# Two transformer blocks on one core: one pass over x for two norm roots, context prepared inside a feed-forward, index scores ordered by head

## The reference, cut to what matters

```python
# block 1
x = x + 0.5 * swiglu(rmsnorm(x, g_ffn1), ...)                     # ffn1
p = rmsnorm(x, g_mix) @ w_in                                      # qa, ka, va, qi, ki, wi, cq, ckv, kr
# index scores: 16 heads of 64 features, three blocks of 128 queries with 256, 384, 512 keys
idx_logits = einsum('bqhd,bsd->bqhs', qib, k_idx)
score = einsum('bqh,bqhs->bqs', wb, relu(idx_logits))             # top-k of it selects keys
q = rmsnorm(c_q, g_q_lat) @ w_uq ; kv = rmsnorm(c_kv, g_kv_lat) @ w_ukv   # value half of kv: VB
out_a = sparse attention (8 heads) ; out_b = latent attention (8 heads)
x = x + concat([out_a, out_b]) @ w_out
x = x + 0.5 * swiglu(rmsnorm(x, g_ffn2), ...)                     # ffn2
x = rmsnorm(x, g_final)                                           # "final"
# block 2
x  = x  + 0.5 * ml[2] * swiglu_2(modulate(rms_norm(x,  norm1_g), ml[0], ml[1]), ...)   # ffn3
cx = cx + 0.5 * mc[2] * swiglu_2(modulate(rms_norm(cx, norm1_g), mc[0], mc[1]), ...)   # same weights
# projections, convolution branch, attention of 8 heads over 768 keys, merge, last feed-forward
```

## Time and profile before

| | us |
|---|---|
| median of 3 runs | 2821.77 (2820.44 to 2825.56) |
| the profiled execution | 2822.73 |
| its span, first to last instruction | 2820.9 |
| mean granted TensorE clock over the span | 0.959 |
| PE busy | 2709.4 |

### The profile page before, as it was taken

One profiled execution on the slowest core, in us unless ns is written; L12 is line 12 of the kernel. 1 busy time (PEld: TensorE's weight loads), 2 busy tenths in 40 slices (PEclk: granted clock), 3 DMA queues, 4 the chain that ended last, 5 costly groups with the idle time before them and its releaser, 6 DMA issues.

```text
span 2820.9 us, 34194 instructions
## 1 busy us (share of the span) xinstructions
PE 2709.4 (96%) x12500; PEld 2168.7 (77%) x12500; DVE 1421.5 (50%) x2491; ACT 757.6 (27%) x1029; POOL 346.7 (12%) x259
## 2 busy tenths in 40 slices
PE   8999989888899999998999999999999999999998
PEld 6888877644457888878888888878888756888887
DVE  7877784556647756673122222254324653433333
ACT  3111232235542112133111111222322352321213
POOL 2111120000002101111211301200200002210102
PEclk9999999869699999987999999999999999999999
DMA  6444432200034454431212221222332001323331
GB/s 181 135 134 144 135 116 74 54 15 1 0 102 115 135 142 147 130 109 37 67 60 60 60 75 56 64 75 90 90 105 83 31 1 60 90 90 98 96 97 67
DMA packets 394763, 241.12 MB, mean 85 GB/s; under 512 B 14768, under 2 KB 392752, under 8 KB 394672
## 3 DMA queue, kind: packets, MB, share of 16 engines
q1 hardware_dynamic: 394672, 239.92, 29.1%
HBM read 237.79 MB, written 2.10 MB: 85 GB/s over the span
## 4 chain that ended last, share of the span: by engine, by line
PE 88%; DVE 7%; ACT 4%; issue 1%; DMA 1%; POOL 0%; SPq 0%; DVEq 0%; ACTq 0%; POOLq 0%
PE PS L669 22%; PE PS L676 21%; PE PS L671 21%; PE PS L656 3%; PE PS L653 3%; PE PS L654 3%; PE PS L1053 2%; PE PS L810 1%; PE PS L610 1%; DVE RB L1414 1%; PE PS L1033 1%; PE PS L896 1%; DVE WL L1361 1%; PE PS L876 1%; PE PS L903 1%
## 5 line engine op out<-in xcount | busy, mean ns | idle before, releaser
L669 PE MATMUL PS<-NH,WH 128*128 128x512 f32 (+1 forms) x2128 | 626.0, 376 | 10.6 <-DVE WL L1361 6.3
L671 PE MATMUL PS<-NH,WL 128*128 128x512 f32 (+1 forms) x2128 | 620.1, 373 | 0.0
L676 PE MATMUL PS<-NL,WH 128*128 128x512 f32 (+1 forms) x2128 | 591.5, 372 | 0.0
L1361 DVE TENSOR_TENSOR WL<-RAW,WH 128x2048 fp32r<-128x2048 f32 x190 | 462.0, 2432 | 103.6 <-ACT WH L1080 103.1
L1080 ACT ACTIVATE WH<-RAW 128x2048 fp32r<-128x2048 f32 x190 | 363.7, 1914 | 540.0 <-PE PS L676 501.0
L669 PEld LDWEIGHTS PS<-NH,WH 128*128 128x128 f32 x2128 | 384.0, 189 | 79.3 <-issue 9.0
L671 PEld LDWEIGHTS PS<-NH,WL 128*128 128x128 f32 x2128 | 389.3, 189 | 72.2
L676 PEld LDWEIGHTS PS<-NL,WH 128*128 128x128 f32 x2128 | 389.5, 189 | 71.9
L1414 DVE SCALAR_TENSOR_TENSOR RB<-MW,CV,RB 128x128 f32<-128x128 f32 x826 | 329.2, 431 | 17.8
L1126 ACT ACTIVATE SA<-PS 128x512 f32<-128x512 f32 x104 | 62.0, 596 | 663.1 <-PE PS L676 630.6
L669 PE MATMUL PS<-HH,WH 128*128 128x512 f32 (+1 forms) x820 | 237.5, 371 | 1.9 <-DVE WL L1361 1.9
(11 more groups left out here) (268 smaller groups left out, 2691.6 us busy)
## 6 DMA issues: line engine op xcount, KB each, us to landing
RAW<-in_ffn_w_in SPq DMA_DIRECT2D x88, 512.0 KB, 4.8
MW<-in_w_mod SPq DMA_DIRECT2D x72, 512.0 KB, 3.7
RAW<-in_w_in SPq DMA_DIRECT2D x70, 512.0 KB, 4.1
RAW<-in_w_gate SPq DMA_DIRECT2D x44, 512.0 KB, 4.2
RAW<-in_w_up SPq DMA_DIRECT2D x44, 512.0 KB, 5.4
RAW<-in_w_down SPq DMA_DIRECT2D x32, 512.0 KB, 4.3
RAW<-in_ffn_w_out SPq DMA_DIRECT2D x32, 512.0 KB, 4.3
RAW<-in_w_out SPq DMA_DIRECT2D x16, 512.0 KB, 4.4
```

The source lines that it names most:

```text
L669: pe.matmul(outs[half][x], w[half][0], xh(k), start=k == 0, stop=False)
L671: pe.matmul(outs[half][x], w[half][1], xh(k), start=False, stop=False)
L676: last = pe.matmul(outs[half][x], w[half][0], xl(k), start=False, stop=k == kn - 1)
L1361: dve.tensor_tensor(WL[1 - s][:, :], RAW[1 - s][:, :], WH[1 - s][:, :].bitcast(F32), ALU.subtract).then_inc(w_lo, 1)
```

## The change

1. *Index scores.* `INDEX` runs over heads outside and the three blocks of queries inside. The products use four banks, the relus three slices of SA. The roots of `norm_q` and `norm_kv` are taken together, their squares during the last projection stages; their spreads stand after index products 2 and 3. VectorE applies both norms and splits the value weights before its first index sum. The value product stands inside the index products, one token block after each of products 24, 26, 28 and 30, in banks 4 and 6, and ScalarE copies it to VB. The clearing of VB and the KB copies go to GpSimd, early.
2. *Between the blocks.* `norm_final` is gone. With y = x r g, the root that ffn3 needs is that of y: ScalarE squares each slice twice, once scaled by the absolute gain (for `norm_x1`, with eps2 = eps squared), once plain (FS); GpSimd adds both. `norm_x1` reads the X of ffn2 with the gain GX. The plain sum gives the final norm's root later: its sums stand after the spread of `norm_x1`, its root after the third high half, its spread before the seventh slice of ffn3's first stage, and VectorE multiplies X by it (`final_applied`) in that stage, with the rest of the `b_mod` additions.
3. *Context.* The squares (two activations with an accumulated sum), transposes, copies and root of the context run in the first four `down` stages of ffn2 (`ctx_work`), its scaling and halves one slice per stage in the second `gate_up` chunk. These stages are written out instead of looped.
4. *Attention.* The value products of a group stand after the scores and before the turn of the next group's first unit, in both attentions.
5. SBUF tiles are placed anew (VB behind QB and KB; FS and FD over unused parts of the hidden tiles).

```diff
+        INDEX = [(q, h) for h in range(IDX_HEADS) for q in range(1, NT)]
+        IX_V = 24
 # TensorE
-            norm(norm_q, v_b)
-            norm(norm_kv, None)
...
+            norm_sums(norm_q, None)
+            norm_sums(norm_kv, None)
+            pe.wait_ge(psum_free, v_b)
+            for n, (q, h) in enumerate(INDEX):
+                if n >= 4:
+                    pe.wait_ge(ix_relu, n - 3)
+                r = slice((h % 2) * 64, (h % 2) * 64 + 64)
+                pe.matmul(B[n % 4][:, 0:(q + 1) * P], QI[r, h // 2, q * P:(q + 1) * P], KI[r, 0:(q + 1) * P],
+                          start=True, stop=True).then_inc(ix_mm, 1)
+                if n == 2:
+                    norm_spread(norm_q, None)
+                elif n == 3:
+                    norm_spread(norm_kv, None)
+                elif n >= IX_V and n % 2 == 0 and n < IX_V + 2 * NT:
+                    values((n - IX_V) // 2)
...
+                if u > 0 and u % PER_GROUP == 0:
+                    heads(u // PER_GROUP - 1)
                 if u >= 0:
                     turn(u)
-                    if u % PER_GROUP == PER_GROUP - 1:
-                        heads(u // PER_GROUP)
+            heads(NG - 1)
...
-            norm(norm_final, ffn3[0][0])
-            pe.wait_ge(ctx_loaded, 16 * (TC // P))
-            for n in range(2 * TC // P):
...
-            norm(norm_c1, None)
-            norm(norm_x1, None)
+            norm_sums(norm_x1, None)
+            norm_spread(norm_x1, ffn3[0][0])
+            pe.wait_ge(f_acc, KD - 1)
+            for t in range(NT):
+                last = pe.matmul(B[4][:, t:t + 1], FS[:, 0, t * P:(t + 1) * P], ones[:, 0:1], start=True, stop=True)
+            last.then_inc(f_mm, 1)
 # ScalarE
+            for n, (q, h) in enumerate(INDEX):
+                act.wait_ge(ix_mm, n + 1)
+                if n >= 3:
+                    act.wait_ge(ix_acc, n - 2)
+                act.activation(SF[:, (n % 3) * T:(n % 3) * T + (q + 1) * P], B[n % 4][:, 0:(q + 1) * P], ACT.Relu)\
+                    .then_inc(ix_relu, 1)
+                if n == 2:
+                    norm_high(norm_q)
+                    norm_high(norm_kv)
...
 # VectorE
+            norm_inverse(norm_q)
+            norm_inverse(norm_kv)
+            norm_apply(norm_q)
+            dve.wait_ge(norm_lo, norm_q.lo + 3)
+            norm_apply(norm_kv)
+            split(v_b % 2, v_b)
+            for n, (q, h) in enumerate(INDEX):
...
+            def final_applied():
+                dve.wait_ge(f_rb, 1)
+                for k in range(KD):
+                    last = dve.scalar_tensor_tensor(out=X[:, k, :], in0=X[:, k, :], scalar=vec("g_final", k), in1=RB[:, :],
+                                                    op0=ALU.mult, op1=ALU.mult)
...
             for b, j, s, at in stage(dve, b0, n, low is not None, lead=2 if b0 == ffn3[0][0] else 0):
+                    if low is not None:
+                        norm_scaled(low, j)
                     mods(b0, j, s, m0)
                     split(s, b)
+                    if low is not None:
+                        norm_low(low, j)
 # GpSimd
+            def final_sum(k):
+                pool.wait_ge(f_sq, k + 1)
+                if k > 1:
+                    pool.wait_ge(f_acc, k - 1)
+                pool.tensor_tensor(FS[:, 0, :], FS[:, 0, :], FS[:, 1 + k % 2, :], ALU.add).then_inc(f_acc, 1)
```

More of the change, by code:

```diff
@@ L622, in norm_spread @@
                         .then_inc(norm_bc, 1)
-                if warm_up:
+                if warm_up and m is not norm_x1:
                     busy(5)
@@ L779, in items, with values @@
                     last.then_inc(rope_mm, 1)
+            def values(t):
+                s = v_b % 2
+                if t == 0:
+                    begin(v_b)
+                    pe.wait_ge(norm_lo, norm_kv.lo + 2)
+                if t >= 2:
+                    pe.wait_ge(v_out, t - 1)
+                for k in range(2):
+                    xh, xl = (z[:, (3, 7)[k], t * P:(t + 1) * P] for z in (NH, NL))
+                    wh, wl = (z[s][:, k * 512:(k + 1) * 512] for z in (WH, WL))
+                    pe.matmul(B[4 + 2 * (t % 2)][:, :], xh, wh, start=k == 0, stop=False)
+                    pe.matmul(B[4 + 2 * (t % 2)][:, :], xh, wl, start=False, stop=False)
+                    last = pe.matmul(B[4 + 2 * (t % 2)][:, :], xl, wh, start=False, stop=k == 1)
+                last.then_inc(v_mm, 1)
             for n in range(10):
@@ new lines, in norm_low @@
+            def norm_low(m, k):
+                if k in m.pooled:
+                    return
+                dve.wait_ge(norm_hi, m.low + k + 1)
+                h, l = m.dst(k)
+                if m.shift:
+                    ins = dve.scalar_tensor_tensor(out=l, in0=scaled(m, k), scalar=m.shift(k),
+                                                   in1=h.bitcast(F32), op0=ALU.add, op1=ALU.subtract)
+                else:
+                    ins = dve.tensor_tensor(l, scaled(m, k), h.bitcast(F32), ALU.subtract)
+                ins.then_inc(norm_lo, 1)
@@ L1431, in gate_up @@
+            def gate_up(b0, n, tok, g0, h0, m0=None, low=None):
+                for b, j, s, at in stage(dve, b0, n, low is not None, lead=2 if b0 == ffn3[0][0] else 0):
+                    if low is not None:
+                        norm_scaled(low, j)
                     mods(b0, j, s, m0)
                     split(s, b)
+                    if low is not None:
+                        norm_low(low, j)
+                    if b0 == ffn3[0][0] and isinstance(j, int) and j == 0:
+                        final_applied()
@@ L1892, in _ @@
             ffn(ffn2, T, H0["ffn2"])
-            norm(norm_final)
+            norm(norm_x1)
+            final_sum(KD - 1)
+            pool.wait_ge(f_r, 1)
+            for t in range(NT):
+                pool.tensor_scalar(FD[:, t * P:(t + 1) * P], ident[:, :], RF[:, t:t + 1], None, ALU.mult).then_inc(f_dg, 1)
             ffn(ffn3, T + TC, H0["ffn3"])
```

356 lines of the change are left out of this document (210 added, 146 removed).

## The result

The changed kernel takes 2753.62 us (median of 4 runs, 2751.96 to 2756.46) against 2821.11 for the kernel before on the same chip: ratio 0.976, 95% interval 0.9743 to 0.9777. The forecast was 2749, so the gain is 68 us where 73 were expected. The profiled execution took 2751.96, its span is 2750.2.

What follows compares the result with a forecast made beforehand. PE, busy 96% of the span, bounds the kernel, so gains are its low-clock or idle time and removed work. 27 + 31 + 9 + 6 = 73 us off 2822.73 gives 2749.7, median 2749; range 2738 to 2758, chance 0.60.

Steps and rivals of the forecast that it cites:

- Part 1: Index scores up to ScalarE's weight copy for `project(0)`: a gain of 27 us, bounds a loss of 3 to 33.
- VectorE's pace: Index scores: VectorE alone needs 1.62 us a head, 26 us for 16 heads; taken for the last eight heads.
- I let the clock rise during it, and stay up: Index scores: PE's clock rises during the value product, from product 24, and stays up.
- the front: Start of the index scores: norm sums, first products and VectorE's norms and value weights put the first index sum at 558.2 us.
- Rival A: Index scores: a head's products run serially; gain 19 instead of 27, or -3; time 2757 to 2779; chance 0.16.
- Part 2: Between the blocks: one pass instead of three gains 36.5 us, net 31 after costs in ffn2 and ffn3; bounds 27 to 34.
- only that of slice 6: Between the blocks: of GpSimd's additions of squares only slice 6's is on the path, as in the kernel before.
- rival C: Feed-forward stages: hidden context and final norm work shows, 16 us come back, time 2765; chance 0.07.
- Part 3: Attentions: later value products fill PE's waits for PT; gains 9 us in block 1 and 6 in block 2.
- the upper bound of 20 for block 1: First attention: the gain could reach 20 us through fewer drops of the clock.
- Rival D: From the index scores on: half-filled array keeps the clock at 1.2 GHz, attentions start low; slower, 2889; chance 0.02.

Runs made afterwards that it cites:

- e10: Changed kernel with the value product from index product 38 on instead of 24: 2753.31 us, ratio 0.9766 to the kernel before.
- e5: Changed kernel with index products ordered so that neighbours are in alternate halves of the array: 2750.06 us, ratio 0.9741 to the kernel before.
- e7: Changed kernel with two banks instead of four for the index scores: 2783.90 us, ratio 0.9864 to the kernel before.
- e6: Changed kernel with 96 unused bytes ahead of HH, which then starts on a multiple of 128: 2743.36 us, ratio 0.9719 to the kernel before.
- e1: Kernel before with one unused tile of 32 bytes per partition ahead of HH, no instruction changed: 2833.77 us against 2819.65, ratio 1.0047.
- e9: Changed kernel with index products in alternating halves and 96 unused bytes ahead of HH: 2738.84 us, ratio 0.971 to the kernel before.
- e4: Changed kernel with the product of heads after the turn of its last unit again, in both attentions: 2776.25 us, ratio 0.9844 to the kernel before.

## Why the prediction was right, and where it was not

**Part 1** (-27, measured -26.1). All times here count from the last projection product. The first index sum was to come after 20.6 us and came after 20.1 (at 561.1); product 24 after 34.5, measured 33.7; value product and index products among it 10.7, measured 10.4; the last part 8.6, measured 10.3. VectorE's pace held. It waits 1.5 us at the start of the last part and then runs 16 sums with no gap above 0.1 us, three of them, one head, in 1.59 us where 1.62 was forecast:

```profile
586.60 0.62 DVE L1717 SCALAR_TENSOR_TENSOR BIAS<-SA,WI,BIAS 128x384 f32<-128x384 f32 x1 [1.17 <-ACT SA L1290]
587.57 8.86 DVE L1717 SCALAR_TENSOR_TENSOR BIAS<-SA,WI,BIAS 128x512 f32<-128x512 f32 x16 [0.35 <-ACT SA L1290]
```

Most of the rest of the difference is one product more in that part (17, not 16).

The step that failed is "I let the clock rise during it, and stay up", said of the value product: e10 shows the rise without any value product. The failure was hidden in the sum. From the first index sum to product 24 the prediction had 13.9 us at 2.45 us a head; it took 13.6, at 2.5 us a head before the clock rose (14 records, seven products, in 5.9 us) and 1.5 after it (25 records in 6.1). Two slips in the front nearly cancel too. The earlier trace rows gives 3.69 ns a column, not 3.33, so the first three products take 4.2 us and not 3.84. The two sets of sums, by their own terms, end at 543.6 and not 542.9; both norms' sums took 4.7 us in all where 5.3 stood in the sum.

Rival A's mechanism, serial products in one half, is real (4.20 against 2.91 us) and costs the 4.3 us that e5 takes back. The Trainium skill, page "TensorE: Matmul & The Clock Gate", section "Part 3: Packing small matmuls — row/col tiling", says that weight loads overlap running products only where the row groups differ; the trace agrees. The serial products did not cost the 8 us of rival A, which had the low clock up to product 24. What the part can't do without are the four banks (e7), which the prediction named only as a condition.

**Part 2** (net -31). Between the blocks -35.3 for -36.5: the step held. PE waits 4.00 us for the sums instead of 2.50, because VectorE is late. Its last two additions to X start 1.2 us after the last product's end (1215.86), where they started 0.2 us ahead of that end before (1248.18), and ScalarE's last square and GpSimd's last addition wait for it.

VectorE is late because GpSimd now adds two sets of squares. The prediction had of these additions "only that of slice 6" on the path; that step failed. In the trace of the changed kernel VectorE's `w_mod` step (L1518) takes 0.34 to 0.64 us where it touches no GpSimd addition (734 of them) and 1.26 to 1.37 where it lies wholly beside one (seven). In the last `down` chunk of ffn2 seven steps so take 6.43 us instead of 4.63, the low half of the weights comes late, and PE waits 1.51 us. The first row is of the kernel before, the others of the changed one:

```profile
1233.02 4.63 DVE L1414 SCALAR_TENSOR_TENSOR RB<-MW,CV,RB 128x128 f32<-128x128 f32 x7
```

```profile
1197.28 6.43 DVE L1518 SCALAR_TENSOR_TENSOR RB<-MW,CV,RB 128x128 f32<-128x128 f32 x7
1205.97 0.50 PE L672 MATMUL PS<-HH,WH 128*128 128x512 f32 x1 [1.51 <-DVE WL L1456]
```

No run takes these additions away, so this cause is read from the traces and not tested.

The parts of ffn2's growth of 6.9 us can be told apart with e6, where HH is on a multiple of 128 as before. The first `down` chunk is 46.6 us there against 44.5, so the context costs 2.1 of the 3 predicted. The last one is 35.6 against 33.8, the 1.8 us of the wait above. Against e6 the three `down` chunks of the changed kernel are 3.4 us longer, which is the addresses (e1 has 2.6 more than before in this stretch with not one instruction changed); the stages between are 0.4 us shorter than before. The prediction would be wrong, it said, if ffn2 grew by more than 5 us. It did, by 6.9, and half of that is the addresses, which the prediction did not have. But e6 with the addresses put right is still 5.0 above the kernel before and e9 3.5, where 3 were predicted. ffn3 is 2.6 longer in e6 for 2.1 predicted. The cover of rival C held but for the 1.8 us.

**Part 3** (-15, measured -26.9) is the term that was mis-sized. The new order cut PE's idle time by 12.3 us (e4), near the 15 that the waits of the earlier trace rows gave. The sum took no change of the clock, though the upper bound of 20 for block 1 named it: 8.0 us of busy time went with the order. The other 6.6 us of the one pair of profiles are busy time at a lower mean clock in the kernel before (0.81 against 0.83, 0.97 against 1.00); 2.8 of them, in the second attention, are not the order's, and for the 3.8 in the first the runs leave it open.

**What no step had.** The prediction costed the moved SBUF tiles at nothing and didn't name them. Their new addresses cost 10 (e6) to 14 us (e1), nearly all of the 12 us that the attentions gave above the forecast. So the total was right within 5 us by luck, with two errors of some 12 in it, and the change with HH on a multiple of 128, as it was before, is worth 78 us (e6). Rival D is refuted in its mechanism too: e10's half-filled products hold the clock at 1.00.

## What to carry to other kernels

Compare code that was not changed first: a stretch with the same instructions and another length is a cause that no argument on the edits will find, and the start to start time of a product shows it. Keep streamed float32r tiles on multiples of 128 bytes when small ones are added ahead of them. For a loop over three engines count the banks before the order: going back to two banks cost 25 us here, the old order of the heads nothing, and neighbours in the same half of the array 4. Work moved to an idle engine is not free if another engine slows down beside it: here VectorE's steps beside GpSimd's additions.

## What the runs showed of the hardware

- A float32r product of 512 streamed columns at the full clock starts 227 ns after the one before it if its streamed tile starts on a multiple of 128 bytes, 233 to 235 ns if it starts 32 or 64 bytes above one. The plain float32 products of the second attention do not show it (twelve records in 5.31 us either way).
- With products that fill half of the array's rows and no gap in PE, the clock rose to 1.00 and stayed there for 14.2 us (e10); with waits of 0.6 us after every three of them it stayed at 0.50 from 562.7 to 589.2 us (e7), the first 1.4 us of a full-array product among them.
- Three such products, of 256, 384 and 512 columns, take 4.20 us in one half at the low clock and 2.91 in alternate halves.
- A VectorE step of 128 by 128 with two tiles read takes 0.35 us, and 1.26 to 1.37 us wholly beside a GpSimd addition of two tiles.
